# A three-stage network in fp32: a rebuilt opening, gate columns one block later, and dummy products in six norms

## The chip, the cores and the metric

One core of one Trainium2 chip. The time is device microseconds from start to end of one execution. Before the change it is 1591.26 us, the median of 3 runs (1588.89 to 1591.47).

## The reference

256 tokens of width 1024, all fp32, through a first block and two layers of a second one. The opening of the first block is what most of the change touches:

```python
def adaln(c, w, b):
    mod = jax.nn.silu(c) @ w + b
    shift, scale, gate = jnp.split(mod, 3, axis=-1)
    return shift[:, None, :], scale[:, None, :], gate[:, None, :]

# first_block
shift, scale, gate = adaln(c, w_ada_mix[i], b_ada_mix[i])
h = rms_norm(x, norm_mix_w[i]) * (1.0 + scale) + shift
x = x + gate * mixer_sublayer(h, w_in[i], ...)
shift, scale, gate = adaln(c, w_ada_ffn[i], b_ada_ffn[i])
h = rms_norm(x, norm_ffn_w[i]) * (1.0 + scale) + shift
x = x + gate * ffn_sublayer(h, w_ffn_in[i], w_ffn_down[i])
return rms_norm(x, final_norm_w)
```

The mixer starts with `h @ w_in` (a gated convolution over 31 taps, a state-space scan). The second block has a delta-rule mixer (projections `h @ w_in` with 32 extra columns for its gates), a gated linear attention, layer norms and two perceptrons.

## The kernel before, in words

**Weights.** Every projection runs through one pipeline. A block is 1 MB of weights (1024 rows by 256 columns), loaded by SyncE (`load`, L400) into one of four buffers `raw`. ScalarE rounds each half block to `whi` (`split_hi`, L420), VectorE or GpSimd takes the rest `wlo = raw - whi` (`split_lo`, L430; the section's `lo` says which engine), and TensorE multiplies three times (L547 to L549): high by high, low activations by high, high by low weights. The first block of a stage behind a norm has an order of its own (`pe_first`, L485, L486, L492): first all products with HH, which it takes tile by tile as ScalarE writes it, then those with HL. The sections `conv_b`, `conv_a`, `xbc`, `z`, `g`, ... follow each other; the order on each engine is the order of the code.

**Modulation.** `silu(c) @ w_ada` is done on VectorE: w_ada is read in 1 MB pieces of 128 rows by 2048 columns, and each piece is multiplied by a column of `cs` and added to `ADA` (`ada_step`, L1371 for the first, L1373 for the rest). TensorE then sums over partitions with a column of ones (`ada_sums`, L2017). Eight pieces for the mixer's shift and scale (`ADA_FIRST`) come before all else, eight for the feed-forward's (`ada_rest`, into `ADA2A`) one behind each block of `conv_b` and `conv_a`. All pieces use the same four `raw` buffers and the same order of loads as the weights; a load waits until the piece or block four places earlier has been used.

**The opening.** ScalarE issues 24 small loads of parameters (`PRW`, L927) and eight more (L928 to L934), TensorE transposes x (L2006) and the parameters (L2012), VectorE copies them to `par` (L1364), ScalarE computes `cs` (L940). Meanwhile the norm's sums are made (`norm_act` L616, `norm_pe` L604). VectorE writes `MOD` (L1387, L1388), then ACC (L652), ScalarE HH (L632), VectorE HL (L666), GpSimd H (`norm_pool`, L674). Only then are the first weights split.

**Gates of the delta-rule mixer.** After block 0 of `a_qkv`, TensorE computes 32 columns (`small_tok`, L2033), ScalarE their sigmoid (`bet`, L1128); behind block 1 VectorE runs a softplus as a chain of small operations (L1424 to L1436, seven of them at L1433). VectorE's other work there is the short convolution behind each block (L1504), which also frees TensorE's accumulators; GpSimd does the low halves of the weights.

**A norm.** TensorE sums over the width with a matrix of ones (`norm_pe`: L599 for the mean, L604 for the squares), ScalarE makes 1/sqrt in two steps, VectorE multiplies (SQX), ScalarE writes HH, VectorE HL. TensorE has nothing between its last sum and the first tile of HH.

## Time and profile before

| | |
|---|---|
| median of 3 runs | 1591.26 us |
| profiled execution | 1588.26 us, its span 1586.2 us |
| TensorE | 1425.9 us busy, 90% of the span |
| VectorE, ScalarE, GpSimd | 964.3, 755.6 and 371.7 us busy |
| mean granted TensorE clock | 0.954 of full speed |
| chain that ended last | PE 74%, DVE 12%, ACT 6%, issue 3% |

Busy shares say that TensorE is nearly always at work; the chain says where it isn't. The two things to look for are stretches in which TensorE stands idle and stretches in which its clock is granted at 0.5.

### The profile page before, as it was taken

The numbers are of one execution on the slowest core, as the hardware profiler recorded it, in microseconds if no ns is written. First come the engines' busy times: TensorE is split into PE (matmuls) and PEld (weight loads), VectorE is DVE, ScalarE is ACT, GpSimd is POOL, SyncE is SP. The second block draws the span as 40 slices with busy tenths as digits, with TensorE's granted clock in tenths as the row PEclk, the third lists the DMA queues.
The fourth block names the chain that finished last, engine by engine and source line by source line (L and its number), as shares of the span: only waits on it lengthen the run. The fifth ranks groups of instructions, "written<-read, shape, count | busy, mean of one in ns | idle before, by whom it ended". The sixth has DMA issues, their size and how long they took to land.

```text
span 1586.2 us, 27900 instructions
## 1 busy us (share of the span) xinstructions
PE 1425.9 (90%) x10968; PEld 1376.1 (87%) x10968; DVE 964.3 (61%) x1641; ACT 755.6 (48%) x1160; POOL 371.7 (23%) x316
## 2 busy tenths in 40 slices
PE   2689999989979999998989888999999987999997
PEld 2689998978979999988889778999988976899996
DVE  4676895746746765459845555765444555666442
ACT  2334555575334333365584444664334644566333
POOL 1216875312500000056543310912002000200000
PEclk7798999999989999999999998999999999999998
DMA  8666554223835754635410004565543410365540
GB/s 292 206 215 211 185 160 133 81 91 123 264 108 190 246 169 147 204 108 159 134 54 1 1 1 133 160 185 178 181 145 109 160 54 2 115 199 185 174 149 27
DMA packets 202473, 223.60 MB, mean 141 GB/s; under 512 B 7611, under 2 KB 197726, under 8 KB 200320
## 3 DMA queue, kind: packets, MB, share of 16 engines
q1 hardware_dynamic: 197232, 220.21, 43.5%
q10 hardware_dynamic: 5135, 1.92, 0.5%
q8 instruction: 73, 1.20, 0.3%
q14 instruction: 33, 0.26, 0.1%
HBM read 221.07 MB, written 1.05 MB: 140 GB/s over the span
## 4 chain that ended last, share of the span: by engine, by line
PE 74%; DVE 12%; ACT 6%; issue 3%; DMA 2%; POOL 1%; ACTq 1%; DVEq 0%; SPq 0%
PE acc L547 18%; PE acc L549 17%; PE acc L548 17%; DVE GB L1504 2%; PE acc L485 2%; PE acc L486 2%; PE acc L492 2%; PE pm L604 1%; ACT whi L420 1%; DVE ADA L1373 1%; DMA raw<-in_w_ffn_in 1%; PE pm L599 1%; PE pm L2017 1%; POOL AM L888 1%; DVE spt L1433 1%
## 5 line engine op out<-in xcount | busy, mean ns | idle before, releaser
L547 PE MATMUL acc<-HH,whi 128*128 128x256 f32 x1728 | 498.3, 288 | 24.5 <-issue 7.4
L420 ACT ACTIVATE whi<-raw 128x1024 fp32r<-128x1024 f32 (+2 forms) x380 | 379.3, 1030 | 290.6 <-PE acc L549 201.7
L548 PE MATMUL acc<-HL,whi 128*128 128x256 f32 x1728 | 493.3, 286 | 0.0
L549 PE MATMUL acc<-HH,wlo 128*128 128x256 f32 x1728 | 493.3, 285 | 0.0
L430 DVE TENSOR_TENSOR wlo<-raw,whi 128x1024 fp32r<-128x1024 f32 (+2 forms) x292 | 337.6, 1188 | 214.2 <-ACT whi L420 211.7
L547 PEld LDWEIGHTS acc<-HH,whi 128*128 128x128 f32 x1728 | 336.3, 195 | 31.7 <-issue 18.3
L548 PEld LDWEIGHTS acc<-HL,whi 128*128 128x128 f32 x1728 | 336.3, 195 | 0.3 <-issue 0.2
L549 PEld LDWEIGHTS acc<-HH,wlo 128*128 128x128 f32 x1728 | 336.0, 194 | 0.0
L430 POOL TENSOR_TENSOR wlo<-raw,whi 128x1024 fp32r<-128x1024 f32 x88 | 216.1, 2475 | 453.0 <-ACT whi L420 449.9
L547 PE MATMUL acc<-HIDH,whi 128*128 128x256 f32 x688 | 195.0, 283 | 6.4 <-ACT whi L420 4.5
L548 PE MATMUL acc<-HIDL,whi 128*128 128x256 f32 x688 | 194.7, 283 | 0.0
L549 PE MATMUL acc<-HIDH,wlo 128*128 128x256 f32 x688 | 194.7, 283 | 0.0
L547 PEld LDWEIGHTS acc<-HIDH,whi 128*128 128x128 f32 x688 | 132.1, 192 | 7.0 <-issue 7.0
L549 PEld LDWEIGHTS acc<-HIDH,wlo 128*128 128x128 f32 x688 | 132.1, 192 | 0.0
L548 PEld LDWEIGHTS acc<-HIDL,whi 128*128 128x128 f32 x688 | 132.1, 192 | 0.0
L674 POOL TENSOR_SCALAR X<-SQX,par 128x256 f32<-128x256 f32 x24 | 30.9, 1302 | 334.2 <-DVE SQX L652 334.2
L485 PE MATMUL acc<-HH,whi 128*128 128x256 f32 x224 | 68.0, 332 | 33.0 <-ACT HH L632 12.1
L485 PEld LDWEIGHTS acc<-HH,whi 128*128 128x128 f32 x224 | 50.8, 227 | 37.4 <-issue 32.6
L1490 DVE SCALAR_TENSOR_TENSOR pm<-UP,par,pm 128x256 f32<-128x256 f32 x158 | 66.9, 480 | 0.0
L486 PE MATMUL acc<-HH,wlo 128*128 128x256 f32 x224 | 64.6, 316 | 0.0
L1255 ACT ACTIVATE TMP<-acc 128x256 f32<-128x256 f32 x64 | 24.6, 384 | 65.3 <-PE acc L549 47.8
L888 POOL TENSOR_TENSOR AM<-ATT,gm 128x512 f32<-128x512 f32 x28 | 38.3, 1389 | 66.8 <-DVE ATT L1793 47.6
(469 smaller groups left out, 2366.0 us busy)
## 6 DMA issues: line engine op xcount, KB each, us to landing
raw<-in_mlp_w SPq DMA_DIRECT2D x64, 1024.0 KB, 5.4
raw<-in_w_in SPq DMA_DIRECT2D x36, 1024.0 KB, 5.4
raw<-in_w_ffn_in SPq DMA_DIRECT2D x22, 1024.0 KB, 5.4
raw<-in_a_w_in SPq DMA_DIRECT2D x16, 1024.0 KB, 5.7
raw<-in_w_ada_mix SPq DMA_DIRECT2D x12, 1024.0 KB, 5.7
raw<-in_w_ada_ffn SPq DMA_DIRECT2D x12, 1024.0 KB, 5.5
raw<-in_b_w_in SPq DMA_DIRECT2D x12, 1024.0 KB, 5.3
raw<-in_w_ssm_out SPq DMA_DIRECT2D x8, 1024.0 KB, 5.2
```

Of the source, the lines that this page charges most:

```text
L420: act.activation(whi[:, (s.t0 + 2 * u + h) % 4, 0:k], raw[:, place(s, b, u) % 4, 0:k, h * P:h * P + P], ACT.Copy).then_inc(hi_ready, 1)
L430: v.tensor_tensor(wlo[:, slot, 0:k], raw[:, place(s, b, u) % 4, 0:k, h * P:h * P + P], whi[:, slot, 0:k].bitcast(F32), ALU.subtract).then_ ...
L485: pe.matmul(acc[:, q, 0:T], whi[:, slot, i], hh, start=i == 0, stop=False)
L486: pe.matmul(acc[:, q, 0:T], wlo[:, slot, i], hh, start=False, stop=False)
L492: m = pe.matmul(acc[:, q, 0:T], whi[:, slot, i], rhs(i)[1], start=False, stop=i == KT - 1)
L547: pe.matmul(acc[:, q, 0:T], whi[:, slot, i], hh, start=first and i == 0, stop=False)
L548: pe.matmul(acc[:, q, 0:T], whi[:, slot, i], hl, start=False, stop=False)
L549: m = pe.matmul(acc[:, q, 0:T], wlo[:, slot, i], hh, start=False, stop=final and i == k - 1)
L674: pool.tensor_scalar(dst[:, k], SQ[name][:, k], shift(k) if shift else 0.0, None, ALU.add)\
L888: pool.tensor_tensor(AM[u][:, lv % 2].rearrange("p (s c) -> p s c", s=4), ATT[u][:], mask, ALU.mult).then_inc(am_ok, 1)
L1490: c.tick(v.scalar_tensor_tensor(ACC[:, i] if w_ == CW - 1 else sum_, src, wt, sums.get(i, sum_), ALU.mult, ALU.add))
L1504: ins = v.scalar_tensor_tensor(d_, x_, pc(w, i + 24 * tap), d_, ALU.mult, ALU.add)
```

## The change

Modulation pieces 0 to 15 get a ring of three buffers of their own (`ADR`, each with a semaphore `ada_in`), apart from `raw`; SyncE issues pieces 0 and 1, then x, then piece 2, five small loads, and pieces 3 to 7, before any weights. Pieces 8 to 15 go behind the weight loads of blocks 2 to 9 (`with_sides`), and the three matrices `ws1` to `ws3` too. `c` is loaded alone, transposed first by TensorE, and ScalarE takes its silu from PSUM ahead of most parameter loads. VectorE copies `par` after the eight steps. The first block of `conv_b` is split inside the norm: `whi` on ScalarE ahead of HH, `wlo` of one half ahead of `MOD`, of the other between ACC and HL. TensorE runs eight products of constants ahead of the modulation's sums. GpSimd's H waits until HL is done. In the norms `ffn`, `final`, `ln1_0`, `ln2_0`, `ln1_1` and `ln2_1` TensorE runs four products of constants behind the sum of squares, and two behind the sum for the mean where there is one. The gate columns of `a_qkv`, their sigmoid and the softplus move one block later.

```diff
-    ADA_PLAN = {"conv_b": (1, 1, 1, 1), "conv_a": (1, 1, 1, 1), "ssm_out": (0, 1, 1, 1, 1, 0, 0, 0),
+    ADA_PLAN = {"ssm_out": (0, 1, 1, 1, 1, 0, 0, 0),
                 "ffn_in": (0, 1, 0, 1, 0, 1, 0, 1) + (0,) * 14}
...
-    order = [("ada", n) for n in range(len(ADA_FIRST))]
+    ADA_SIDE, ADA_RING = 16, 3
+    order = []
...
-        s.hi_ahead = s.name != "conv_b"
-        s.lo_done = s.ahead or s.name in ("conv_out", "ffn_in")
+        s.hi_ahead = True
+        s.lo_done = s.ahead or s.name in ("conv_b", "conv_out", "ffn_in")
...
+        ADR = [ar(f"ADR{i}", (46, 54, 38)[i], [P, 2 * D]) for i in range(ADA_RING)]
...
             def load_ada(n):
                 name, b = (ADA_FIRST + ADA_REST)[n]
+                if n < ADA_SIDE:
+                    if n >= ADA_RING:
+                        sp.wait_ge(ada_used, n - ADA_RING + 1)
+                    sp.dma_start(ADR[n % ADA_RING][:], ada_src(name, b)).then_inc(ada_in[n % ADA_RING], 16)
+                    return
...
+            def with_sides(s, b, u, j):
+                load(s, b, u, j)
+                if not s.flat:
+                    return
+                w = s.w0 + b
+                if 2 <= w < 10:
+                    load_ada(8 + w - 2)
+                if w in SIDES:
+                    w_, src, off, done = SIDES[w]
+                    sp.dma_start(w_[:], src.rearrange("(k p) c -> p k c", p=P)[:, :, off:off + NH]).then_inc(done, 16)
+            SIDES = {3: (ws1, w_in, OFF_DT, dt_in), 6: (ws2, a_in, A_BA, x_in), 8: (ws3, b_in, B_GL, x_in)}
...
+        def keep_busy(pe, n):
+
+            for _ in range(n):
+                pe.matmul(pm[:, 2, 0:T], ones, maskf[:, 0:T], start=True, stop=True)
+
         def norm_pe(pe, name):
...
                 m.then_inc(n_mean, 1)
+                keep_busy(pe, 2)
...
             m.then_inc(n_sum, 1)
+            if name not in ("mix", "conv"):
+                keep_busy(pe, 4)
...
             pool.wait_ge(mod0_ok, 1)
+            pool.wait_ge(n_hl, 8)
...
+            act.dma_start(CIN[:], vec(a["c"][0])).then_inc(c_in, 16)
+            act.preload_act_table_set("silu_and_others")
+            for n, (ap, p0, i, m) in enumerate(pieces):
+                if n == 4:
+                    act.wait_ge(c_p, 1)
+                    act.activation(cs[:], pm[:, 2, 0:DT], ACT.Silu).then_inc(silu_c, 1)
+                    act.preload_act_table_set("natural_log_exp_and_others")
                 act.dma_start(PRW[p0:p0 + m, i, :], ap).then_inc(par_in, 16)
...
-            act.wait_ge(par_ok, 2)
-            act.activation(cs[:], pc("c", 0, 8), ACT.Silu).then_inc(silu_c, 1)
-            norm_act(act, "mix", mod_col(0))
+
+            def conv_b_hi():
+                for h in range(2):
+                    split_hi(act, SEC["conv_b"], 0, 0, h)
+            act.wait_ge(ada_used, 1)
+            norm_act(act, "mix", mod_col(0), between=conv_b_hi)
...
+            for bk in range(2):
+                v.wait_ge(par_t, bk + 1)
+                m = min(512, NPAR - 512 * bk)
+                v.tensor_copy(par[:, 512 * bk:512 * bk + m], pm[:, 2 * bk, 0:m]).then_inc(par_ok, 1)
+            split_lo(v, SEC["conv_b"], 0, 0, 0)
             v.wait_ge(ada_sum, 1)
...
-            norm_dve(v, "mix", mod_col(8), mod_col(0))
+            norm_dve(v, "mix", mod_col(8), mod_col(0), lambda: split_lo(v, SEC["conv_b"], 0, 0, 1))
...
             def qkv_more(b):
-                if b == 1:
+                if b == 2:
                     gates()
...
+            pe.wait_ge(c_in, 16)
+            pe.transpose(pm[:, 2, 0:DT], CIN[:], ident[0:DT, 0:DT]).then_inc(c_p, 1)
             pe.wait_ge(x_in, 16)
...
-            norm_pe(pe, "mix")
+            for _ in range(8):
+                pe.matmul(acc[:, 3, 0:T], ones, maskf[:, 0:T], start=True, stop=True)
             pe.wait_ge(ada_part, 1)
             ada_sums(16, ADA, ada_sum)
...
             def gates(b):
-                if b == 0:
+                if b == 1:
                     pe.wait_ge(n_t, 8 * NORM["final"][0] + 8)
+                    pe.wait_ge(x_in, 16 * 3)
                     small_tok(ws2, SQX, ba_p)
```

(TensorE's norm sums for `mix` stand, in the change, between the transposes of x and those of the parameters.) Three places, as the built programs order them. First, SyncE's queue from the program's start, before and then in the change; ADR_93 to ADR_95 are the three buffers of the ring.

```order
L363 DMA XIN<-in_x 128x2x1024
L383 DMA raw<-in_w_ada_mix 128x2048 x8
L400 DMA raw<-in_w_in 128x8x256
L383 DMA raw<-in_w_ada_ffn 128x2048
L400 DMA raw<-in_w_in 128x8x256
```

```order
L388 DMA ADR_93<-in_w_ada_mix 128x2048
L388 DMA ADR_94<-in_w_ada_mix 128x2048
L397 DMA XIN<-in_x 128x2x1024
L388 DMA ADR_95<-in_w_ada_mix 128x2048
...
L388 DMA ADR_94<-in_w_ada_mix 128x2048
L419 DMA raw<-in_w_in 128x8x256 x3
L388 DMA ADR_95<-in_w_ada_ffn 128x2048
L419 DMA raw<-in_w_in 128x8x256
```

x went from first to third, and four blocks of weights now stand ahead of all but one of the later pieces. Second, VectorE from the last modulation step to the first later piece, before and then in the change.

```order
L1373 SCALAR_TENSOR_TENSOR ADA<-raw,cs,ADA 128x2048 [waits ada_used,landed3]
L1387 TENSOR_TENSOR MOD<-pm,par 128x16 [waits ada_used,ada_sum]
L1388 SCALAR_TENSOR_TENSOR MOD<-MOD,par 128x8 [waits vchain]
...
L666 SCALAR_TENSOR_TENSOR HL<-ACC,MOD,HH 128x256 [waits norm_hh] x8
L1396 MEMSET UP 128x8x30
L430 TENSOR_TENSOR wlo<-raw,whi 128x1024 [waits w_used,landed0,hi_ready,raw_used,vchain]
L430 TENSOR_TENSOR wlo<-raw,whi 128x1024 [waits hi_ready,w_used]
```

```order
L1423 COPY par<-pm 128x512 [waits ada_used,par_t]
L1423 COPY par<-pm 128x155 [waits par_t]
L461 TENSOR_TENSOR wlo<-raw,whi 128x1024 [waits hi_ready,w_used,landed0]
L1427 TENSOR_TENSOR MOD<-pm,par 128x16 [waits par_ok,ada_sum]
...
L691 SCALAR_TENSOR_TENSOR ACC<-X,MOD,NR 128x256 x7
L461 TENSOR_TENSOR wlo<-raw,whi 128x1024 [waits hi_ready,w_used]
L705 SCALAR_TENSOR_TENSOR HL<-ACC,MOD,HH 128x256 [waits norm_hh] x8
L461 TENSOR_TENSOR wlo<-raw,whi 128x1024 [waits hi_ready,w_used,landed1]
```

One half split now stands ahead of MOD, one ahead of HL, and the copies of `par` behind the eight steps. Third, ScalarE in `a_qkv`, before and then in the change; GB is the output of the short convolution.

```order
L1117 ACTIVATE GB<-acc,par 128x256 [waits w_used] x2
L1128 ACT_TABLE_LOAD
L1128 ACTIVATE bet<-pm 128x32 [waits ba_p]
L1130 ACTIVATE X<-SQX 128x2048
L420 ACTIVATE whi<-raw 128x1024 [waits w_used,landed0]
L420 ACTIVATE whi<-raw 128x1024 [waits w_used]
```

```order
L1155 ACTIVATE GB<-acc,par 128x256 [waits w_used] x2
L1165 ACTIVATE X<-SQX 128x2048
L451 ACTIVATE whi<-raw 128x1024 [waits w_used,landed1]
L451 ACTIVATE whi<-raw 128x1024 [waits w_used]
L1155 ACTIVATE GB<-acc,par 128x256 [waits w_used] x2
L1168 ACT_TABLE_LOAD
L1168 ACTIVATE bet<-pm 128x32 [waits ba_p]
L1171 ACT_TABLE_LOAD
L1171 ACTIVATE spt_69<-spt_68 128x32 [waits sp_x]
L451 ACTIVATE whi<-raw 128x1024 [waits w_used,landed2]
```

The split of block 2 no longer stands behind the wait for the gate columns (`ba_p`); the split of block 4 stands behind both that one and the softplus's (`sp_x`).

## Rows read from the trace of the kernel before

**Rows 1.** The page: the span, and the clock granted in 40 slices.
```profile
span 1586.2 us, 27900 instructions
PEclk7798999999989999999999998999999999999998
```

**Rows 2.** Timeline of the opening: start us, us, engine, line, operation, tiles, count, idle before and its releaser.
```profile
6.20 3.68 PE L2006 MATMUL acc<-ident,XIN 128*128 128x128 f32 x16 [6.20 <-POOLq L848]
...
18.59 1.58 PE L2012 MATMUL pm<-ident,PRW 128*128 128x128 f32 x6 [8.72 <-DMA PRW<-in_ln_b]
...
22.47 0.21 ACT L940 ACTIVATE cs<-par 128x8 f32<-128x8 f32 x1
...
22.78 1.29 DVE L1371 TENSOR_SCALAR ADA<-raw,cs 128x2048 f32<-128x2048 f32 x1 [2.04 <-issue]
...
24.18 17.08 DVE L1373 SCALAR_TENSOR_TENSOR ADA<-raw,cs,ADA 128x2048 f32<-128x2048 f32 x7
24.46 5.21 PE L604 MATMUL pm<-ACC,maskf 128*128 128x256 f32 x16 [4.29 <-ACT ACC L616]
...
41.37 6.98 PE L2017 MATMUL pm<-maskf,ADA 128*128 128x1 f32 x32 [11.70 <-DVEq L1385]
```

**Rows 3.** Same timeline, from the modulation's sums to the end of block 0.
```profile
48.93 3.84 DVE L652 SCALAR_TENSOR_TENSOR ACC<-X,MOD,NR 128x256 f32<-128x256 f32 x8 [0.16 <-DVE MOD L1388]
52.68 4.13 DVE L666 SCALAR_TENSOR_TENSOR HL<-ACC,MOD,HH 128x256 fp32r<-128x256 f32 x8
57.10 4.81 DVE L430 TENSOR_TENSOR wlo<-raw,whi 128x1024 fp32r<-128x1024 f32 x4
58.72 0.55 PE L485 MATMUL acc<-HH,whi 128*128 128x256 f32 x1 [10.37 <-issue]
...
63.93 2.08 PE L492 MATMUL acc<-HL,whi 128*128 128x256 f32 x16
```

**Rows 4.** Stretches: us, busy us by engine (PE, PEld, DVE, ACT, POOL), PEclk, DMA share, GB/s.
```profile
5.00:10.00 5.00, 3.68 (x16) 3.28 (x16) 0.00 (x0) 0.00 (x0) 0.89 (x4) 1.00 1.03 422
25.00:30.00 5.00, 4.67 (x16) 3.55 (x14) 4.79 (x3) 1.84 (x7) 0.00 (x0) 0.75 1.00 362
45.00:50.00 5.00, 3.36 (x16) 3.27 (x16) 1.42 (x5) 0.55 (x2) 0.40 (x1) 0.50 0.48 193
```

**Rows 5.** DMA issues of the first 60 us, the load of x: KB each, us from issue to landing.
```profile
XIN<-in_x SPq DMA_DIRECT2D x1, 1024.0 KB, 4.9
```

**Rows 6.** The chain in order of time, `conv_b` to `xbc`: start us, us, what.
```profile
83.29 3.49 PE pm L2033 x32
...
96.64 7.61 DMA raw<-in_w_in
```

**Rows 7.** Timeline of TensorE: the start of `xbc`, and block 4 of `a_qkv`.
```profile
117.56 0.58 PE L547 MATMUL acc<-HH,whi 128*128 128x256 f32 x1 [4.80 <-DVE UP L1418]
...
721.78 0.55 PE L547 MATMUL acc<-HH,whi 128*128 128x256 f32 x1 [5.11 <-DVE GB L1504]
```

**Rows 8.** Timeline of VectorE and GpSimd: seven softplus steps at each place, and GpSimd's splits.
```profile
109.95 1.78 DVE L1433 SCALAR_TENSOR_TENSOR spt<-spt,spt 128x64 f32<-128x64 f32 x7
...
708.38 9.97 DVE L1433 SCALAR_TENSOR_TENSOR spt<-spt,spt 128x32 f32<-128x32 f32 x7
...
708.18 9.45 POOL L430 TENSOR_TENSOR wlo<-raw,whi 128x1024 fp32r<-128x1024 f32 x4 [3.95 <-ACT whi L420]
```

**Rows 9.** Stretches of 2 us: behind the stall in `a_qkv`, and behind `ln1_1`.
```profile
722.00:724.00 2.00, 2.00 (x10) 2.00 (x11) 1.86 (x6) 0.33 (x1) 0.00 (x0) 0.50 0.20 71
1376.00:1378.00 2.00, 2.00 (x10) 2.00 (x10) 2.00 (x5) 1.88 (x6) 2.00 (x3) 0.50 0.00 0
```

**Rows 10.** Timeline of TensorE: first product behind `ffn`; sum and first product of `ln1_1`.
```profile
476.58 0.55 PE L485 MATMUL acc<-HH,whi 128*128 128x256 f32 x1 [5.60 <-ACT HH L632]
...
1369.96 3.72 PE L604 MATMUL pm<-SQX,maskf 128*128 128x256 f32 x16 [0.96 <-ACT SQX L616]
1375.85 0.55 PE L485 MATMUL acc<-HH,whi 128*128 128x256 f32 x1 [2.16 <-ACT HH L632]
```

More of the change, by code:

```diff
@@ L158, in program @@
             for _ in range(ADA_PLAN.get(s.name, (0,) * s.nb)[b]):
-                s.ada[b].append(sum(k == "ada" for k, _ in order))
+                s.ada[b].append(ADA_SIDE + sum(k == "ada" for k, _ in order))
                 order.append(("ada", s.ada[b][-1]))
@@ L165, in program @@
     for s in SECS:
-        s.hi_ahead = s.name != "conv_b"
-        s.lo_done = s.ahead or s.name in ("conv_out", "ffn_in")
-    ADA_AT = [i for i, (k, _) in enumerate(order) if k == "ada"]
-    assert len(ADA_AT) == len(ADA_FIRST) + len(ADA_REST)
+        s.hi_ahead = True
+        s.lo_done = s.ahead or s.name in ("conv_b", "conv_out", "ffn_in")
+    ADA_AT = {n: i for i, (k, n) in enumerate(order) if k == "ada"}
+    assert len(ADA_AT) + ADA_SIDE == len(ADA_FIRST) + len(ADA_REST)
+    for i in range(4):
+        SEC["conv_b"].ada[i].append(8 + i)
+        SEC["conv_a"].ada[i].append(12 + i)
     for a_, b_ in zip(SECS, SECS[1:]):
@@ L290, in program @@
         vchain, achain, gchain = sem("vchain"), sem("achain"), sem("gchain")
-        par_in, x_in = sem("par_in"), sem("x_in")
+        par_in, x_in, dt_in = sem("par_in"), sem("x_in"), sem("dt_in")
+        ada_in = [sem(f"ada_in{i}") for i in range(ADA_RING)]
+        ws1 = ar("ws1", 91, [P, DT, NH])
+        ws2 = ar("ws2", 92, [P, DT, NH])
+        ws3 = ar("ws3", 93, [P, DT, NH])
         masks = sem("masks")
         par_t, par_ok = sem("par_t"), sem("par_ok")
-        silu_c = sem("silu_c")
+        silu_c, c_in, c_p = sem("silu_c"), sem("c_in"), sem("c_p")
         ada_part, ada_sum, mod_ok = sem("ada_part"), sem("ada_sum"), sem("mod_ok")
@@ L1360, in _ @@
             c.link(v.memset(sc[:, 1:2], LN_EPS))
-            for bk in range(2):
-                v.wait_ge(par_t, bk + 1)
-                n = min(512, NPAR - 512 * bk)
-                v.tensor_copy(par[:, 512 * bk:512 * bk + n], pm[:, bk, 0:n]).then_inc(par_ok, 1)
-            v.wait_ge(par_ok, 2)
+            c.link(v.memset(UP[:, :, 0:CW - 1], 0.0))
             v.wait_ge(silu_c, 1)
@@ L2007, in _ @@
                 m.then_inc(xt_p, 1)
+            norm_pe(pe, "mix")
+            pe.wait_ge(silu_c, 1)
             pe.wait_ge(par_in, 16 * len(pieces))
@@ L2011, in _ @@
                     n = min(P, NPAR - P * i)
-                    m = pe.transpose(pm[:, bk, (i % 4) * P:(i % 4) * P + n], PRW[0:n, i, :], ident[0:n, 0:n])
+                    m = pe.transpose(pm[:, 2 * bk, (i % 4) * P:(i % 4) * P + n], PRW[0:n, i, :], ident[0:n, 0:n])
                 m.then_inc(par_t, 1)
```

64 lines of the change are left out of this document (32 added, 32 removed).

## The prediction

> **What bounds the kernel now.** I read the page first: the span is 1586.2 us, and the row of granted clocks has its lowest digits in the first two of 40 slices, 7 and 7, with a scatter of 8s and 9s behind [rows 1]. Then the timeline from the start. TensorE's first product of weights begins at 58.72 us [rows 3], and before that it does only transposes and sums. What it waits for is one chain: the last of the 24 parameter loads lands at 18.59, they are transposed and copied, ScalarE has `cs` at 22.47 + 0.21, VectorE makes the modulation's eight steps from 22.78 to 41.26 (1.29, then seven in 17.08, one every 2.45 us), and TensorE's sums take 6.98 us more [rows 2]. Behind them come ACC 3.84 us, HL 4.13 us and the first split, 4.81 us for four halves, 1.2 each [rows 3]. That none of this had to wait for `cs` so late is seen in the loads: x lands 4.9 us after its issue [rows 5], and the DMA moves 422 GB/s from 5 to 10 us [rows 4], 1 MB each 2.5 us. The later places to look at are TensorE's idle times with an engine's name behind them: 4.80 us at the start of `xbc`, 5.11 us in block 4 of `a_qkv` [rows 7], and the idle time in the norms, 5.60 us in `ffn` and 2.16 us in `ln1_1` [rows 10].
>
> **The opening, step by step.** `c` alone should land before 6.20 us, where TensorE starts because GpSimd has its masks ready [rows 2]; one transpose and the silu of 0.21 us put `cs` at about 6.9 instead of 22.7. VectorE can then start 16 us earlier, but now the loads set its pace. Pieces 0 and 1 land at about 5.7 and 8.2 (4.9 us behind the issue at 0.8, and 2.5 more), x at 10.7, piece 2 at 13.3, and then a piece each 2.5 us, since a buffer of three is free again one step after its use and the engines of the DMA are full: piece 7 lands at about 26.1. VectorE's eighth step ends at 28.5, 12.8 us earlier than 41.26. I cost the wait for a ring of three at nothing beyond this: a free buffer comes back after a load of 4.9 us and a step of 2.45 with some 0.5 of issue, 7.9 us for three steps, 2.6 each.
>
> TensorE has by then: x transposed from 10.8 (3.68 us), the norm's sums from about 19.9, when ScalarE is through with its loads (some 16.0) and its copies of x (5.21 us), the parameters' transposes (1.58 us), and eight products of constants. These take 3.72/8 = 0.47 us each [rows 10] at the full clock, 0.93 at half. In the same sums of before the clock rose some 3 us after their start, which is the 0.75 in the stretch from 25 to 30 us [rows 4]; so I take it as full, and the eight products end at about 30.3, 1.7 us after VectorE's last step. The sums then take 3.49 us, as the same number of thin products did at the full clock [rows 6], where before they took 6.98 at 0.50 [rows 4]: MOD is there at about 34.3 instead of 48.8, 14.5 us earlier.
>
> Behind MOD VectorE does ACC (3.84 us at most; GpSimd, which now waits, ran beside it), one split of 1.2, and HL (4.13 at most): 9.2 us instead of ACC, HL and all the first splits. TensorE starts with ACC's first tiles, about 35, and is paced by them. From 58.72 TensorE needed until 65.9 for block 0, where the last sixteen products end [rows 3]; now it ends when HL does and a last 1 us, near 44 instead of 65.9. That is **22 us** at the end of block 0. The weights' split of block 0 is hidden: its `whi` waits for a load that lands at 28.6, its first `wlo` runs while TensorE sums.
>
> In `conv_b` and `conv_a` TensorE needs 5.76 us a block (48 matmuls of 0.12) and 3.49 us for the first gate columns; that is unchanged. Before, it also waited once for weights that were issued behind a modulation piece and took 7.61 us to land [rows 6], 1.8 us, and 4.80 us at the start of `xbc` for VectorE, which was held by the softplus and a step. With a ring of its own the first goes; loads are issued three blocks ahead. What is late next is VectorE: in `conv_a` a block costs it 2.4 of splits, 0.8 of products and 2.45 of a step, 5.6 us against 5.76, and on top of that 6.5 us of small operations. It starts with about as much backlog as before, so I leave 4 to 5 us of waiting at the start of `xbc`. I take **24 us** for the whole opening. Bounds: 18, if MOD comes as the rival of the cold sums has it, to 30, if all of the waits go.
>
> **Gate columns.** Before, the chain of seven steps at L1433 took 9.97 us where the same seven took 1.78 elsewhere: GpSimd was in four splits for 9.45 of them [rows 8]. VectorE came 8 us late to the evacuations, and TensorE waited 5.11 us [rows 7] and ran at 0.50 for about 5 us behind that [rows 9], another 2.5. One block later, ScalarE's split of block 2 no longer waits for the gate columns, so GpSimd's splits are not bunched into four; but the split of block 4 waits for the sigmoid and the softplus's first step, so TensorE waits 1 to 1.5 us there. 5.1 + 2.5 − 1.5 gives **6 us**. Bounds: 8, and 0 if the collision comes again. The Trainium skill (SBUF — State Buffer, SBUF: two separate sides) states that GpSimd and a VectorE instruction with two SBUF inputs exclude each other for a whole instruction, whoever starts first; by that rule moving the chain cures nothing unless GpSimd happens to be idle.
>
> **Six norms.** Four products take 1.86 us at the full clock and stand in an idle time of 2.16 us (5.60 in `ffn`), so they delay nothing; at half clock they would take 3.7. The two behind the mean, 0.93 us, fit the 0.96 us before the squares [rows 10]. What they can save is the half clock that follows: 0.50 from 1376 to 1378, although TensorE was at work again since 1375.85 [rows 9, 10]. But the products there are paced by the tiles of HH and HL on VectorE, so only a little of it is on the path: I take 1.3 us in `final`, a few tenths in the others, together **2 us**, with bounds −8 (the fill late in five norms, 1.5 us each) and +5 (`ffn` kept at the full clock too, 3 us). The Trainium skill (TensorE: Matmul & The Clock Gate, Part 1) says that half rate is the default and that only activity releases it; by that rule too little filling would leave the clock where it was, and the 2 us would be 0.
>
> **The sum.** 1588.26, the profiled execution's own time, less 24, 6 and 2 is 1556.3. The median of the runs stands 3.0 above the profiled execution, so I predict **1559.3 us**. A measurement of this kernel can tell about 0.2%, 3 us, from no change.
>
> **Rivals.**
> *Cold sums.* TensorE stands still between the norm's sums and its eight products because the parameter loads, 8 us later in ScalarE's queue than before, land late (they landed last at 18.59 while the DMA was full). Then the eight products run at half clock, 3.7 us longer, and stand in front of the modulation's sums, which may take 6.98 instead of 3.49. For it: 0.50 is what the sums of before had [rows 4]. Against it: the last loads should land near 25, when TensorE ends the norm. 7 us less, 1566.
> *The stall in `a_qkv` only moves.* GpSimd's split of block 4 starts at the same moment as the softplus. The chain is then stuck for 5 us again, and the 6 us are lost: 1565.
> *The fill harms.* At half clock the four products outlast the idle time, 1.5 us in each of five norms, and the 2 us don't come: 1559.3 + 9.5 = 1569.
> *The ring starves, slower.* SyncE's queue is in order: each of pieces 8 to 15 waits for a step on VectorE, with the next block of weights queued behind it. If VectorE frees a buffer more than about 10 us after the weights' buffer, each such wait ends in a late load of 7.61 us [rows 6], some 5 us on the path: 8 × 5 = 40 us on top of the forecast, 1599. It decides only if the wait for the ring exceeds the lead of three blocks, 17 us; I find it 2 to 3 us behind the other one.
> *The change does nothing:* `c` doesn't land early, since its 4 KB share the DMA with full 1 MB loads. Then `cs` comes at 18 or so and the opening gains a few us only: 1583.
>
> **How the numbers follow.** Forecast 0.55, cold sums 0.15, moved stall 0.13, harmful fill 0.08, starved ring 0.03, late `c` 0.06 (half of it within 0.2%). The range takes in the bounds of the parts, 44 us at best for all of them together (1547), and three of the rivals: 1548 to 1573. Faster 0.94, same 0.03, slower 0.03.
>
> **What would show it.** Right: VectorE's first step at 7 us and the last ending near 28.5; TensorE's thin sums in about 3.5 us; its first product of weights at about 35; `xbc` starting near 93 instead of 117.56; seven L1433 steps of 2 us in `a_qkv` and no idle time over 2 us there; granted clock of 1.00 through the six norms. Wrong: a first step near 18, sums of 7 us, idle time of TensorE on DMA in `conv_b` or `conv_a`, or first products behind the norms more than 2.3 us after the last true sum.

## The result, and the profile after

| | before | after |
|---|---|---|
| median of the runs | 1590.65 us (4 runs) | 1575.49 us (4 runs, 1571.33 to 1577.58) |
| ratio after / before | | 0.9902, 95% interval 0.9881 to 0.9922 |
| profiled execution, span | 1588.26, 1586.2 us | 1576.73, 1574.7 us |

The change is faster by 15 us (12 to 19), half of the 32 us that were forecast; the median lies 2.5 us above the range, which ended at 1573. A repeat beside two of the experiments gave 0.9892 (0.9874 to 0.9910), 1575.27 us over six runs from 1569.72 to 1578.80, as close to the first as its text below expects. One execution of the kernel before in the rounds of that repeat took 3504.38 us, in the slow state, and is in no ratio.

The page of after answers to [rows 1]: the first digit of the clock's row is 9 where it was 7, the second 8 where it was 7.

```profile
span 1574.7 us, 28063 instructions
...
PE 1445.0 (92%) x11049; PEld 1391.6 (88%) x11049; DVE 965.7 (61%) x1641; ACT 756.4 (48%) x1160; POOL 380.3 (24%) x316
...
PEclk9889999999899999999999999999999999999999
```

The opening's timeline (columns as in [rows 2]; the rows of VectorE, then of TensorE):

```profile
6.82 1.29 DVE L1405 TENSOR_SCALAR ADA<-ADR,cs 128x2048 f32<-128x2048 f32 x1 [5.39 <-ACT cs L967]
...
14.11 2.35 DVE L1407 SCALAR_TENSOR_TENSOR ADA<-ADR,cs,ADA 128x2048 f32<-128x2048 f32 x1 [3.37 <-DMA ADR<-in_w_ada_mix]
20.11 2.35 DVE L1407 SCALAR_TENSOR_TENSOR ADA<-ADR,cs,ADA 128x2048 f32<-128x2048 f32 x1 [3.65 <-DMA ADR<-in_w_ada_mix]
...
31.01 2.35 DVE L1407 SCALAR_TENSOR_TENSOR ADA<-ADR,cs,ADA 128x2048 f32<-128x2048 f32 x1 [0.23 <-DMA ADR<-in_w_ada_mix]
...
33.48 6.48 PE L2064 MATMUL pm<-maskf,ADA 128*128 128x1 f32 x32 [3.58 <-DVEq L1419]
...
41.69 0.55 PE L516 MATMUL acc<-HH,whi 128*128 128x256 f32 x1 [1.74 <-ACT HH L671]
...
104.75 0.58 PE L578 MATMUL acc<-HH,whi 128*128 128x256 f32 x1 [9.07 <-DVE UP L1461]
...
711.77 0.55 PE L578 MATMUL acc<-HH,whi 128*128 128x256 f32 x1 [5.18 <-DVE GB L1547]
```

The first step is where it was forecast, at 6.8 us. VectorE then waits 3.37 us for piece 2 and 3.65 for piece 3 (used at 20.11, where the forecast has it soon after 15.8), the last step ends at 33.36 instead of 28.5, and the sums take 6.48 us. The last two rows answer to [rows 7]: the wait at the start of `xbc` is 9.07 us, not 4.80, and the stall in `a_qkv` is still there, 5.18 us, one block later.

How far the changed kernel is ahead at each place, in the two profiled executions:

| TensorE is at | before | after | ahead |
|---|---|---|---|
| first product of weights | 58.72 | 41.69 | 17.0 |
| start of `xbc` | 117.56 | 104.75 | 12.8 |
| first product behind `ffn` | 476.58 | 462.84 | 13.7 |
| first product behind the gate sums of `a_qkv` (L2178, L2227) | 772.49 | 756.46 | 16.0 |
| span | 1586.2 | 1574.7 | 11.5 |

So the opening made the gain and had lost 4 us of it again by `xbc`; the rest of the program gave nothing that stands out of the scatter of the clock. The table is one execution against one. The repeat's profiled execution, of the same kernel, starts its first product at 41.80 but `xbc` at 109.82, only 7.7 us ahead of the kernel before, and is 8.6 ahead at `ffn`, 10.9 behind the gate sums and 9.5 at the end. What differs is GpSimd's H of `mix`: 18.16 us in the first, 20.76 in the repeat, where TensorE waits for it and has the half clock behind it, from 70 to 80 us:

```profile
69.18 6.34 PE L2080 MATMUL pm<-ws,H 128*128 128x32 f32 x32 [2.25 <-POOL H L713]
```

The next rows show how the loss at `xbc` comes about, which both executions have (9.07 us); VectorE's and GpSimd's rows of after:

```profile
90.31 1.74 DVE L1470 TENSOR_SCALAR spt<-spt 128x64 f32<-128x64 f32 x1
92.08 0.55 DVE L1471 RECIPROCAL spt<-spt 128x64 f32<-128x64 f32 x1
92.67 1.77 DVE L1472 TENSOR_TENSOR spt<-spt,spt 128x64 f32<-128x64 f32 x1
94.48 2.31 DVE L1473 TENSOR_TENSOR spt<-spt 128x64 f32<-128x64 f32 x1
...
97.05 3.85 DVE L1476 SCALAR_TENSOR_TENSOR spt<-spt,spt 128x64 f32<-128x64 f32 x7
...
103.95 0.74 DVE L1461 TENSOR_TENSOR UP<-acc,G 128x256 f32<-128x256 f32 x2
...
89.58 7.12 POOL L461 TENSOR_TENSOR wlo<-raw,whi 128x1024 fp32r<-128x1024 f32 x3 [23.16 <-DVE wlo L461]
96.92 2.34 POOL L461 TENSOR_TENSOR wlo<-raw,whi 128x1024 fp32r<-128x1024 f32 x1 [0.22 <-ACT whi L451]
```

The rows from L1470 on are the softplus, a chain in which each instruction needs the one before. It took 4.1 us before (108.40 to 112.49) and takes 11.3 now (90.31 to 101.65), with GpSimd in its splits until 99.26. Before, the weights of `xbc` came late, and GpSimd began behind the chain:

```profile
108.40 0.18 DVE L1427 TENSOR_SCALAR spt<-spt 128x64 f32<-128x64 f32 x1
...
112.26 0.23 DVE L1436 SCALAR_TENSOR_TENSOR dtt<-spt,spt 128x64 f32<-128x64 f32 x1
...
112.32 6.73 POOL L430 TENSOR_TENSOR wlo<-raw,whi 128x1024 fp32r<-128x1024 f32 x2 [54.44 <-ACT whi L420]
```

So the repair of the loads made the collision: with weights on time GpSimd starts 0.7 us ahead of the chain instead of with its end. That it is the splits that hold the chain is tested below, by `chain_in_psum`.

### The profile page after: what moved, and what is told of

Read it like the earlier page. It is cut to its first block, busy times and chain, and to the rows that moved or that the text cites. A ratio compares the mean times of both kernels' runs of the same rounds, so it can differ in the third digit from the quotient of the medians.

```text
span 1574.7 us, 28063 instructions
## 1 busy us (share of the span) xinstructions
PE 1445.0 (92%) x11049; PEld 1391.6 (88%) x11049; DVE 965.7 (61%) x1641; ACT 756.4 (48%) x1160; POOL 380.3 (24%) x316
## 4 chain that ended last, share of the span: by engine, by line
PE 76%; DVE 11%; ACT 6%; DMA 3%; issue 2%; POOL 1%; DVEq 0%; SPq 0%; ACTq 0%
PE acc L578 18%; PE acc L580 18%; PE acc L579 18%; PE acc L516 2%; DVE GB L1547 2%; PE acc L517 2%; PE acc L523 2%; DMA ADR<-in_w_ada_mix 2%; PE pm L641 1%; ACT whi L451 1%; DMA raw<-in_w_ffn_in 1%; PE pm L635 1%; PE pm L2064 1%; POOL AM L924 1%; DVE spt L1476 1%
```

## The experiments

All kernels, with the places that tell them apart. H is GpSimd's H of `mix` (eight tiles), the wait is TensorE's at the start of `xbc`; both of the profiled execution. The labels count the edits loosely: `five_edits` and `seven_edits` have six each, `eight_edits` seven. A line added to a kernel moves the line numbers behind it: L1477 of one kernel is L1476 of another.

| kernel | median us | ratio to before (95%) | first product | H took | wait | `xbc` starts |
|---|---|---|---|---|---|---|
| after, first time | 1575.49 | 0.9902 (0.9881–0.9922) | 41.69 | 18.16 | 9.07 | 104.75 |
| `unchanged` (after again) | 1575.27 | 0.9892 (0.9874–0.9910) | 41.80 | 20.76 | 9.07 | 109.82 |
| `small_late` | 1572.68 | 0.9865 (0.9839–0.9891) | 37.72 | 20.93 | 9.07 | 105.89 |
| `sixteen_products` | 1573.70 | 0.9876 (0.9859–0.9893) | 38.92 | 20.76 | 9.07 | 105.30 |
| `ring_of_four` | 1570.54 | 0.9852 (0.9830–0.9874) | 41.53 | 18.20 | 9.07 | 104.65 |
| `chain_in_psum` | 1565.05 | 0.9824 (0.9808–0.9840) | 38.97 | 18.23 | 3.89 | 96.93 |
| `before_chain_in_psum` | 1588.82 | 0.9984 (0.9969–0.9999) | 58.78 | 8.28 | 3.46 | 118.25 |
| `gates_back` | 1570.49 | 0.9854 (0.9834–0.9874) | 39.62 | 18.04 | 9.07 | 102.56 |
| `no_fill` | 1577.02 | 0.9903 (0.9886–0.9919) | 38.34 | 18.18 | 9.07 | 101.12 |
| `three_edits` | 1564.44 | 0.9832 (0.9810–0.9853) | 38.00 | 20.76 | 3.89 | 99.20 |
| `softplus_behind` | 1568.23 | 0.9858 (0.9838–0.9877) | 41.21 | 18.21 | 0.52 | 95.78 |
| `five_edits` | 1562.88 | 0.9825 (0.9806–0.9843) | 39.13 | 20.76 | 0.52 | 98.65 |
| `pool_at_once` | 1571.22 | 0.9861 (0.9838–0.9885) | 41.26 | 10.21 | 9.07 | 106.57 |
| `seven_edits` | 1555.88 | 0.9771 (0.9751–0.9792) | 37.91 | 17.95 | 0.52 | 92.22 |
| `eight_edits` | 1552.89 | 0.9750 (0.9734–0.9766) | 38.56 | 10.21 | 0.52 | 92.29 |

A kernel's own runs lie up to 12 us apart (`pool_at_once`, 1565.04 to 1576.69), so a difference of two medians under about 4 us is read here from the places, not from the medians. The places scatter too. In the twelve profiled executions in which H is made behind HL it took either 17.95 to 18.23 us, and TensorE waited for none of it, or 20.76 to 20.93 (`unchanged`, `small_late`, `sixteen_products`, `three_edits`, `five_edits`), and TensorE waited 2.25 us and had less than the full clock for 6 to 11 us behind it. After itself stands in both groups, so it is not the edits that make the difference, and `xbc` can be compared only within a group.

**The softplus chain (`chain_in_psum`, `before_chain_in_psum`).** One line, in the changed kernel and in the one before:

```diff
         pm = psum("pm", [P, 4, 512])
+        spt[1] = pm[:, 2, 256:320]
```

> One of the four small tiles of the softplus (the one that the seven steps write and read) is put into PSUM, so these steps have one input in SBUF instead of two. Theory, they collide with GpSimd's weight splits over SBUF inputs: the chain before xbc takes 4 to 6 us instead of 11.3, TensorE's wait at the start of xbc falls from 9.1 to 2 to 4 us; in a_qkv the seven steps take 2 us instead of 7.95 and the wait of 5.2 us goes; the kernel is 8 to 13 us faster than the changed one (1562 to 1567). Rival, VectorE's chain is slowed by its own semaphores or its order: times within 1 us of the changed kernel at both places.

> The kernel before, with one edit: the second of the four small buffers of the softplus chains (64 columns) lies in a free corner of the PSUM bank of the small sums instead of in SBUF, so that most of the chain's steps on VectorE have one operand in SBUF instead of two. Theory (a chain of two-operand steps on VectorE and GpSimd's splits shut each other out): in the kernel before this collision stood in `a_qkv` alone (seven steps in 9.97 us there, 1.78 in the opening). So here the seven steps in `a_qkv` take 2 to 4 us, the wait of 4.80 us at the start of `xbc` stays within 1 us of what it was, and the whole gains 3 to 6 us, against 28 us for the same edit in the changed kernel's neighbourhood of 10 us: the changed kernel had made a second collision of its own at `xbc`. Rival (the edit is good for the same 10 us anywhere, since it saves VectorE's time everywhere): 10 us faster here too, with the wait at `xbc` down to 1 us.

(The 28 us in the second text is what the edited changed kernel gains on the kernel before; on the changed kernel it gains 10.) In the changed kernel (VectorE, GpSimd, TensorE at `xbc` and in `a_qkv`):

```profile
88.78 0.67 DVE L1474 TENSOR_TENSOR spt<-spt 128x64 f32<-128x64 f32 x1
...
89.74 1.83 DVE L1477 SCALAR_TENSOR_TENSOR pm<-pm,spt 128x64 f32<-128x64 f32 x7
...
86.95 7.12 POOL L462 TENSOR_TENSOR wlo<-raw,whi 128x1024 fp32r<-128x1024 f32 x3 [23.18 <-DVE wlo L462]
...
96.93 0.58 PE L579 MATMUL acc<-HH,whi 128*128 128x256 f32 x1 [3.89 <-DVE UP L1462]
...
707.14 0.38 PE L579 MATMUL acc<-HH,whi 128*128 128x256 f32 x1 [3.71 <-DVE GB L1548]
```

The chain at `xbc` fell back to 4.7 us (87.67 to 92.36) with GpSimd still in its splits from 86.95 on, the wait from 9.07 to 3.89, and the whole by 10 us. The theory had the stall in `a_qkv` gone too; it fell from 5.18 to 3.71 only, since two of the decay columns behind the chain now meet GpSimd's splits (2.42 and 2.40 us instead of 0.28). So the two waits account for 6.7 of the 10 us; where the rest comes from isn't shown. In the kernel before, VectorE and GpSimd in `a_qkv`:

```profile
707.08 1.60 DVE L1434 SCALAR_TENSOR_TENSOR pm<-pm,spt 128x32 f32<-128x32 f32 x7
...
709.40 4.57 DVE L1700 SCALAR_TENSOR_TENSOR gd<-gd,gab 128x16 f32<-128x16 f32 x2
...
706.86 9.43 POOL L431 TENSOR_TENSOR wlo<-raw,whi 128x1024 fp32r<-128x1024 f32 x4 [3.82 <-ACT whi L421]
```

Seven steps in 1.60 us where [rows 8] had 9.97, inside the very same four splits of GpSimd; the two products behind them, which still have both operands in SBUF, take 4.57 instead of 0.38. So it is the operands that decide, and not the place. The Trainium skill (SBUF — State Buffer, SBUF: two separate sides) states that a GpSimd instruction and a VectorE instruction with two SBUF inputs, or in a two-port mode, shut each other out for a whole instruction. The runs agree: 1.60 us with one input in PSUM, 9.97 with both in SBUF. The whole gains only 2.5 us there (0.1 to 4.9), less than the 3 to 6 expected: TensorE's stall shrank from 5.11 to 3.53 us only (one block later, at 732.00), since the two products and three of the decay columns behind them (2.4 us each) collided in the chain's place. The wait at `xbc`, expected to stay within 1 us of 4.80, was 3.46. The rival, the same 10 us in both kernels, is out.

**The small loads (`small_late`).** The five loads of `dt_bias` and the like move from ahead of piece 3 to behind a block of weights (SyncE's block 3):

```diff
             load_ada(2)
-            sp.dma_start(dtb[:, 0:NH], bcast(a["dt_bias"][0], NH)).then_inc(dt_in, 16)
...
+                if w == 3:
+                    sp.dma_start(dtb[:, 0:NH], bcast(a["dt_bias"][0], NH)).then_inc(dt_in, 16)
```

> The five small loads (dt_bias, a_log, d_skip and two more, 128 descriptors each) go from SyncE's queue ahead of modulation piece 3 to behind the weights of block 3. Theory 1, they are what starves the ring: no stretch of half-empty DMA from 12 to 16 us, VectorE's eighth step ends near 29 us instead of 33.4, TensorE's thin sums then follow its eight products without a pause and take 3.5 us instead of 6.5, its first weight product is near 34 to 35 us instead of 41.7, and the kernel is 4 to 7 us faster than the changed one (1569 to 1571). Rival, three buffers are too few: the eighth step still ends after 32 us with waits on pieces 3 to 7, and the time stays within 2 us of 1575.5.

The stretches of after, and VectorE's steps without the five loads:

```profile
12.00:14.00 2.00, 2.00 (x12) 2.00 (x10) 0.00 (x0) 0.00 (x0) 0.00 (x0) 1.00 0.55 185
14.00:16.00 2.00, 1.06 (x5) 0.66 (x4) 1.89 (x1) 0.00 (x0) 0.00 (x0) 1.00 0.56 168
```

```profile
13.67 2.35 DVE L1408 SCALAR_TENSOR_TENSOR ADA<-ADR,cs,ADA 128x2048 f32<-128x2048 f32 x1 [2.99 <-DMA ADR<-in_w_ada_mix]
16.38 2.35 DVE L1408 SCALAR_TENSOR_TENSOR ADA<-ADR,cs,ADA 128x2048 f32<-128x2048 f32 x1 [0.35 <-DMA ADR<-in_w_ada_mix]
...
28.01 2.35 DVE L1408 SCALAR_TENSOR_TENSOR ADA<-ADR,cs,ADA 128x2048 f32<-128x2048 f32 x1 [0.38 <-DMA ADR<-in_w_ada_mix]
```

With 64 KB of small loads in the queue the DMA ran at 185 and 168 GB/s for 4 us; without them piece 3 is used at 16.38 instead of 20.11, and the last step ends at 30.36 instead of 33.36. So 3.0 of the 4.9 us by which the steps were late are these loads. Of the other 1.9, 0.4 is piece 2 (used at 13.67, landed at 13.3 in the forecast) and the rest the pieces' pace: 2.9 us each from 13.67 to 28.01, not 2.5, with the DMA's share at 1.00 or above in every 2 us from 8 to 32. TensorE still stands idle for 2.98 us ahead of its sums, which take 5.50 us and not 3.5. The first product of weights comes 4 us earlier. `xbc` starts 3.9 us earlier than in the repeat, which has the same wait of 2.25 us for H and a half clock behind it, and no earlier than in the first execution of after, which has none. The time, 1572.68, is not told from the repeat's 1575.27.

**What TensorE does ahead of the sums (`sixteen_products`).** `range(8)` in front of the sums becomes `range(16)`.

> The changed kernel with sixteen products of constants ahead of the modulation's sums instead of eight. Theory (the idle time of 3.58 us between the eight products and the sums is what takes the granted clock away in the sums): sixteen products end at about 33.7, 0.2 us behind the last step; the sums take 3.5 us instead of 6.48, the first product of weights starts 2.5 to 3 us earlier than 41.69, and block 0 runs at the full clock, another 1 to 3 us; 2 to 6 us faster in all, less what the wait at the start of `xbc` gives back. Rival (the clock falls there whatever is done): the sums still take over 5 us, and the time is the same within 3 us.

```profile
26.54 7.17 PE L2067 MATMUL acc<-maskf 128*128 128x256 f32 x32
33.55 3.63 PE L2064 MATMUL pm<-maskf,ADA 128*128 128x1 f32 x32
...
66.30 4.49 PE L2080 MATMUL pm<-ws,H 128*128 128x32 f32 x32 [2.25 <-POOL H L713]
```

The sums take 3.63 us and the first product starts 2.8 us earlier: as the theory had it. The time is the same within the scatter, as the rival had it, but the rival's reason is out. A part of the reason is in the last row: TensorE now comes to the small products of L2080 before GpSimd has H, waits 2.25 us and runs at half clock behind (0.50 or 0.51 in each stretch from 70 to 76 us). `small_late` has that wait too; so has the repeat of after, and against that one `xbc` starts 4.5 us earlier here. The early opening doesn't bring the wait: `gates_back` and `no_fill` start their first product at 39.62 and 38.34, with H in 18.0 and 18.2 us, and have none.

**The ring (`ring_of_four`).** A fourth buffer.

> The changed kernel with a ring of four buffers for the modulation's pieces 0 to 15 instead of three. Theory (the loads set the pace of the eight steps by what the DMA moves, not by how soon a buffer is free): the last of the eight steps ends within 1 us of 33.36, the time is the same within 3 us. Rival (the ring of three starves): piece 3 no longer waits behind the first step, the last step ends 2 to 3 us earlier, and in `conv_b` and `conv_a` no load is late; 3 to 6 us faster.

First product 41.53, `xbc` 104.65, first product behind `ffn` 462.63 against 462.84, last modulation step over at 33.24 against 33.36: the same to 0.2 us for 460 us, so the ring of three starves nothing here. (With the small loads out of the way a fourth buffer was not tried; there the DMA's share says that it is full.) The median is 4.7 us under the repeat's, with intervals that touch; what the two profiled executions differ by comes later, where the edit changes nothing and the granted clock falls in other places: 0.5 us at 711, 1.3 at 1070, 5.9 at 1461. I take it for scatter, and as a warning about medians 5 us apart.

**The gate columns (`gates_back`).** The three conditions `b == 1`, `b == 2`, `b == 1` of ScalarE, VectorE and TensorE go back by one block.

> The gate columns of a_qkv, their sigmoid and the softplus go back to where they were, one block earlier. Theory, the move only carried the collision with it: a wait of 5 us at block 4 instead of block 5, the section within 2 us, time 1575 to 1578. My forecast's step: 6 us slower, 1581.

```profile
686.64 9.98 DVE L1476 SCALAR_TENSOR_TENSOR spt<-spt,spt 128x32 f32<-128x32 f32 x7
...
700.05 0.55 PE L578 MATMUL acc<-HH,whi 128*128 128x256 f32 x1 [5.12 <-DVE GB L1547]
```

In after the same chain takes 7.95 us and 2.27 for the next step, and TensorE waits 5.18: the move shifts the stall and leaves its size. The kernel without the move is 5 us faster in the median (0.9854 against 0.9892, intervals touching), below the 1575 to 1578 that were expected. But its profiled execution is 4.9 us ahead of after's already at the first product behind `ffn` (457.92 and 462.84), over 200 us ahead of the edit's place. So the move gained nothing; that it cost something is not shown.

**The fills (`no_fill`).** Both calls of `keep_busy` are gone.

> The products of constants in the six norms are taken out (their results are read by nobody). Theory, they are worth next to nothing because the products behind a norm are paced by VectorE's and ScalarE's tiles: the granted clock falls to 0.5 behind the norms again, ffn and final are 0.7 and 1.0 us longer, the layer norms the same within 0.3, time within 3 us of the changed kernel. Rival of the forecast, they save 2 us or more in the sum: 1577.5 or more.

1577.02 against 1575.27: no difference. In `ffn` TensorE stands still 5.60 us instead of 3.87, about the length of the fill: it stood in idle time and delayed nothing. The clock did answer. Without the fills it falls behind `final`, `ln2_0` and `ln1_1` (the three stretches below) and behind `ln1_0`; with them it is 1.00 behind these four norms:

```profile
682.00:684.00 2.00, 2.00 (x11) 2.00 (x11) 0.00 (x0) 1.25 (x2) 1.53 (x1) 0.50 1.02 325
1174.00:1176.00 2.00, 2.00 (x10) 1.92 (x10) 2.00 (x6) 0.98 (x2) 2.00 (x3) 0.50 0.13 34
1358.00:1360.00 2.00, 2.00 (x10) 2.00 (x10) 2.00 (x5) 1.88 (x6) 2.00 (x3) 0.50 0.00 0
```

From the first product behind `ffn` to the end the two profiled executions take the same time all the same, 1111.9 us with the fills and 1112.0 without.

**Repeat, and VectorE's order at `xbc` (`unchanged`, `softplus_behind`).**

```diff
                 elif b == 2:
-                    softplus(0, spt[0][:, 0:2 * NH], dtt[:])
...
+                for n in {2: [], 3: [14, 15]}.get(b, SEC["conv_a"].ada[b]):
```

(the softplus goes in front of the logs of block 3).

> The changed kernel once more, as it is, on the chip and in the rounds of the two kernels it is compared with here. It gives what the two below are measured against: all theories expect a ratio to the kernel before within 0.002 of 0.9902. If it comes out near 0.986, a part of what the edits so far seemed to gain (5 us for the gate columns put back, 5 for the ring of four) is the spread between chips and between runs and not the edits.

> The changed kernel with VectorE's order altered at one place: the softplus and the step on piece 14, which stand between the evacuations of block 2 and of block 3 of `conv_a`, stand behind those of block 3. Theory (VectorE has too much to do there, so the wait is only as good as what is queued next): TensorE goes from `conv_a` to `xbc` with a wait under 1 us instead of 9.06, xbc starts at about 96.5 instead of 104.75, but VectorE is then busy with the softplus, the logs and two steps until about 114 and TensorE waits again once its accumulators are full, from about 108: 4 to 6 us come back, and 2 to 4 us remain as a gain. Rival (the accumulators last): no second wait over 1 us in `xbc`, 7 to 9 us faster.

The repeat's ratio is within 0.001 of the first. In `softplus_behind` the wait at `xbc` is 0.52 us, and 5.49 us come back at 107.54, as the theory had it. The ratio is 0.9858 against 0.9892, 5 us: 3.1 of them are the waits (9.07 less 0.52 and 5.49), the rest is not shown to come from the edit. The new order moved the wait more than it removed it: the two steps that now stand last take 6.74 us, beside GpSimd's splits from 105.09 on:

```profile
92.42 0.42 DVE L1461 TENSOR_TENSOR UP<-acc,G 128x256 f32<-128x256 f32 x1 [2.46 <-PE acc L580]
...
103.85 6.74 DVE L1407 SCALAR_TENSOR_TENSOR ADA2A<-ADR,cs,ADA2A 128x2048 f32<-128x2048 f32 x2 [0.23 <-DVE dsk L1499]
...
105.09 12.38 POOL L461 TENSOR_TENSOR wlo<-raw,whi 128x1024 fp32r<-128x1024 f32 x4 [6.19 <-ACT whi L451]
```

**Edits together (`three_edits`, `five_edits`).** Buffer in PSUM, gates back, small loads behind piece 7; then also the order above, the gate columns' softplus into PSUM, twelve products.

> The changed kernel with three edits at once: the softplus chain's second buffer in PSUM, the gate columns back in block 0 of `a_qkv`, and the five small loads behind piece 7 of the modulation instead of ahead of piece 3. Theory (the three losses are separate): first weight product at about 37 instead of 41.69, wait at the start of `xbc` under 5 us, xbc at about 94 instead of 104.75, no wait over 3 us in `a_qkv`; 12 to 18 us faster than the changed kernel, so a ratio to the kernel before of 0.979 to 0.983. Rival (what is gained in the opening is taken back by VectorE's backlog before `xbc`): like the edit of the buffer alone, ratio 0.982 to 0.985.

> The three edits (softplus buffer in PSUM, gate columns in block 0, small loads behind piece 7) with three more: the softplus and the step of piece 14 behind the evacuations of block 3 of `conv_a`; the result of the gate columns' softplus in PSUM, so that the two products behind it have one SBUF operand (they took 4.57 us in the kernel before with its chain in PSUM, 0.38 elsewhere); and twelve products of constants ahead of the sums instead of eight. Theory: the softplus is now short (5 us), so VectorE is through at about 106 and there is no second wait in `xbc`; the wait of 3.89 at the start of `xbc` falls under 1, the first weight product starts at about 37 with the clock at 1.00; 3 to 6 us faster than the three edits, ratio 0.979 to 0.982. Rival (what is gained is given back by a wait in `xbc`): the same as the three edits within 2 us, ratio 0.983.

Both rivals won: 1564.44 and 1562.88, as the buffer alone. `three_edits` starts its first product at 38.00, waits 2.25 us for H, 3.89 at `xbc` and 3.53 in `a_qkv`; `five_edits` waits 2.25 for H, runs at less than the full clock for 10 us behind it, and pays 5.35 us at 110.41. But in `a_qkv` its stall is gone: the two products behind the chain take 0.38, and no wait of TensorE there exceeds 1.5 us.

**GpSimd's H (`pool_at_once`), and what is left (`seven_edits`, `eight_edits`).** The change had made GpSimd wait for HL:

```diff
             pool.wait_ge(mod0_ok, 1)
-            pool.wait_ge(n_hl, 8)
             norm_pool(pool, "mix", mod_col(0), H)
```

`seven_edits` is `five_edits` with the step of piece 14 back in its place (the 2.46 us of idle time shown above); `eight_edits` is that and the line above.

> The changed kernel with the wait of GpSimd for VectorE's last tile of HL taken out again, so that GpSimd makes H beside ACC and HL as in the kernel before. Theory (GpSimd's H was pushed into the stretch in which VectorE does steps and splits without a gap, where it takes 18 to 21 us for eight tiles against 8.28 before; where TensorE gets there first it waits 2.24 us and runs at half clock for up to 10 us behind it): H takes 8 to 10 us and ends before 52; ACC and HL together take 1 to 1.5 us more (3.84 and 4.13 before, 3.25 and 3.25 now); TensorE waits for no H in front of the small products, the clock from 66 to 80 us is 1.00, and the products of block 0 end 1 us later; 1 to 4 us faster in the median, since in some of the executions TensorE doesn't wait today. Rival (H is hidden anyway, ACC and HL are on the path): 1 to 2 us slower.

> As the five edits, but only the softplus and the logs stand behind the evacuations of block 3 of `conv_a`; the step of piece 14 is back between those of blocks 2 and 3, where VectorE was idle for 2.46 us in front of each evacuation. Theory (the second wait, 5.34 us at 110.42, came of two steps of 3.4 us each that stood last): the wait falls to 2 us or less, no other comes, 2 to 4 us faster than the five edits, ratio 0.980 to 0.981. Rival (the step in its old place delays the evacuations): a wait of 2 us or more at the start of `xbc`, same time as the five edits.

> The kernel with seven edits and GpSimd's H made at once, as in `pool_at_once`. Theory: in the kernels with an early opening TensorE reaches the small products before H is there each time (2.25 us at 64.27 with five edits, then half clock until about 77); with H early that wait and the half clock go, 4 to 6 us, less 1 us for ACC and HL: 3 to 5 us faster than the seven edits, ratio 0.976 to 0.979. Rival (the clock falls at that place for another cause, or VectorE gives the time back before `xbc`): same as the seven edits within 2 us.

The timeline's row of GpSimd's H, in three kernels: before, after and `pool_at_once`.

```profile
49.60 8.28 POOL L674 TENSOR_SCALAR H<-ACC,MOD 128x256 f32<-128x256 f32 x8 [43.51 <-DVE ACC L652]
```

```profile
48.26 18.16 POOL L713 TENSOR_SCALAR H<-ACC,MOD 128x256 f32<-128x256 f32 x8 [42.14 <-DVE HL L705]
```

```profile
40.76 10.21 POOL L713 TENSOR_SCALAR H<-ACC,MOD 128x256 f32<-128x256 f32 x8 [34.64 <-DVE ACC L691]
```

H falls from 18–21 to 10.21 us and ends at 51, ACC and HL cost 3.84 and 4.13 again, and TensorE waits for it no more. The half clock behind the small products came all the same in that kernel (0.50 from 72 to 76), so the wait is not its only cause; the time, 0.9861 against 0.9892, is not told from the repeat's. `seven_edits` has no wait of TensorE over 0.6 us between 38 and 130 us and is 7 us faster than `five_edits`, more than the 2 to 4 that were expected. A part of that may be H again, 17.95 us in the one profiled execution and 20.76 in the other, with no edit between them that touches it. VectorE, GpSimd and TensorE of `eight_edits` at the same place as the rows of after above:

```profile
86.40 3.84 DVE L1407 SCALAR_TENSOR_TENSOR ADA2A<-ADR,cs,ADA2A 128x2048 f32<-128x2048 f32 x1
...
92.15 0.22 DVE L1470 TENSOR_SCALAR pm<-spt 128x64 f32<-128x64 f32 x1
...
95.22 1.83 DVE L1476 SCALAR_TENSOR_TENSOR pm<-pm,spt 128x64 f32<-128x64 f32 x7
...
85.68 11.53 POOL L462 TENSOR_TENSOR wlo<-raw,whi 128x1024 fp32r<-128x1024 f32 x4 [37.41 <-DVE wlo L462]
...
92.29 0.39 PE L579 MATMUL acc<-HH,whi 128*128 128x256 f32 x1 [0.52 <-DVE UP L1461]
```

It starts `xbc` at 92.29, keeps the clock at 1.00 from 60 to 80 us, alone among the fourteen profiled executions with the new opening, and takes 1552.89 us: 38.7 us faster than the kernel before, 0.9750 (0.9734 to 0.9766), and 22 faster than the change as made. That it beats `seven_edits` by 3 us is likely but not shown, since the intervals overlap and both profiled spans are 1550.3.

## Why the prediction was wrong

Its direction was right, and so were most of its places; it had the gain twice too large. The profiled sum was 24 + 6 + 2 = 32; the two profiled executions give 11.5, the medians 15 to 16.5. (The parts' best bounds, 30, 8 and 5, add up to 43 and not 44; nothing hangs on it.)

*The opening, 24 us: measured 12.8 at the start of `xbc`.* Three terms of its working failed.
- "VectorE's eighth step ends at 28.5": it ended at 33.36. The step "a piece each 2.5 us" left out the five small loads that the change puts between pieces 2 and 3: they stood at nothing, without a reason. They measure 3.0 us (`small_late`), and most of the other 1.9 is the pace, 2.9 us a piece.
- The sums, 3.49 taken and 6.48 measured, the rival of the *cold sums*, but not by its mechanism. The parameters were in time and the eight products ran at the full clock (26.17 to 29.89); it was the steps, late by 4.9 us, that left TensorE idle for 3.58 us. Sixteen products, which bridge that time, gave 3.63. One error made the other.
- "I leave 4 to 5 us of waiting at the start of `xbc`": 9.07. I had named VectorE as late next and counted its instructions at the durations of before. Where GpSimd would be at that time I had not asked, though the collision stood in [rows 8], and in my own text for `a_qkv`. 5 us, shown by `chain_in_psum`.

What came as forecast: `c` early, the first step at 6.82 (*the change does nothing* is out), the first product 1.3 us behind MOD (0.7 in the forecast), HL's tiles as the pace, block 0 over at about 50 with 15.7 us of the 22. The ring of three starved nothing.

Not in the forecast at all: GpSimd's H, pushed behind HL into a stretch in which VectorE has two-operand work nearly without a gap, takes 18 to 21 us. I had noted that GpSimd "now waits" and booked only what that saves VectorE. At 18 us it costs TensorE no wait, at 21 one of 2.25 us with a longer half clock behind it; with that, the repeat's `xbc` starts 5 us later than the first execution's.

*Gate columns, 6 us: 1.1 by the places, and nothing by `gates_back`.* TensorE is 14.9 us ahead at the end of the first block behind `final` (677.93, 692.83 before) and 16.0 behind the gate sums. "5.1 + 2.5 − 1.5" rested on GpSimd's splits not coming in a bunch; there are still four, with 0.95 us between the pairs, from 698.12 to 708.52 around the chain. The bound of 0 and the rival *the stall only moves* were right, and the sentence beside them, that moving the chain cures nothing unless GpSimd is idle, said why.

*Six norms, 2 us: nothing measurable.* The products delayed nothing, and the clock stayed at 1.00 behind four of the six norms, as forecast. Behind `ffn` (0.54 and 0.61 from 464 to 468) and `ln2_1` (0.50 from 1568 to 1570) it fell all the same. None of this shortened anything that could be measured: the term of 2 us came to 0.1 between the two profiled executions (1112.0 and 1111.9 us behind `ffn`). The bounds of −8 and +5 weren't touched, and *the fill harms* is out. The one place that got slower, the gate logits behind `ln2_0` with 5.17 us instead of 3.64, at a clock of 0.57 from 1184 to 1188, has 3.64 again in the repeat.

The range failed because cases that I had set as alternatives came together, and all on one side: sums 3 us longer, the stall moved (6), the fills worth nothing (2), and with them the two that had no case of their own, the small loads (3) and the collision at `xbc` (5). These are 19 us for the 16 by which the median missed the forecast; read from single executions, the terms are not exact to 3 us.

## What to carry to other kernels

When transfers get earlier, look up what the other engine does with them: here weights on time brought GpSimd's splits onto VectorE's softplus, and the wait there took 5 us of the gain back. A chain of small VectorE instructions that can meet GpSimd's work belongs with one operand in PSUM; with that, an order in which each step falls into an idle time, and H and the small loads moved (`eight_edits`), the same change gave 39 us instead of 15. An edit that gains 3 us at its own place may show nothing in the median. Compare places, one after the other, and first see by a repeat how far a place moves by itself: here `xbc` moved by 5 us between two executions of one kernel.
